# Sample attention: who loads the pages, when the choice of blocks and two exponentials run, and when the first output weights are asked for

## The reference

```python
s_c = einsum(qg, kc); p_c = masked_softmax(s_c)        # compressed branch, 127 tokens a sequence
imp = where(causal, where(forced, 1e9, einsum(p_c, sel_map)), NEG)
_, idx = lax.top_k(imp, 16)                            # choice: 16 of 33 blocks of 64 tokens
o_s = softmax(qg @ K[idx]) @ V[idx]                    # selected branch, pages through page_table
o_w = softmax(qg @ K_win) @ V_win                      # window of 512
o = g[0] * o_c + g[1] * o_s + g[2] * o_w
h = x + concat(o, o_rwkv) @ w_out
```

## Time and profile before

| | |
|---|---|
| median of 3 runs | 2213.54 us (2210.96 to 2214.94) |
| the profiled execution's own time | 2216.07 us |
| its span, first to last instruction | 2214.3 us |
| PE busy | 2114.0 us (95%) |
| mean granted clock of TensorE | 0.976 of full |
| sample attention, first turn to first product of the output projection | 1111.76 to 1242.97 us of the span |

### The profile page before, as it was taken

The page is one execution under the profiler, slowest core; times in us unless marked ns, Lnnn a source line. Parts: engine busy times, 40 slices in busy tenths (PEclk is TensorE's granted clock), DMA queues, the critical chain, the costliest instruction groups (busy, mean ns, idle before and its releaser), DMA issues.

```text
span 2214.3 us, 37125 instructions
## 1 busy us (share of the span) xinstructions
PE 2114.0 (95%) x15276; PEld 1199.3 (54%) x15276; DVE 1130.4 (51%) x2310; ACT 627.7 (28%) x1411; POOL 150.8 (7%) x248
## 2 busy tenths in 40 slices
PE   8999999899998998999987899999999999999999
PEld 6445556799996784444443444444444444444443
DVE  2035654467665547776555114453635455453635
ACT  5014542222222125766643222202011111111020
POOL 3000000122221001212100000000000000000000
PEclk9999999999997997999988899999999999999999
DMA  6001113101012621000045320111111111111112
GB/s 177 37 0 29 29 28 100 50 4 23 4 23 79 199 69 54 10 6 10 1 148 158 99 101 33 38 38 38 38 38 38 38 38 38 38 38 38 39 38 81
DMA packets 99958, 115.73 MB, mean 52 GB/s; under 512 B 32243, under 2 KB 72116, under 8 KB 99726
## 3 DMA queue, kind: packets, MB, share of 16 engines
q1 hardware_dynamic: 95310, 106.01, 15.2%
q10 hardware_dynamic: 4480, 7.34, 1.2%
HBM read 104.75 MB, written 12.64 MB: 53 GB/s over the span
## 4 chain that ended last, share of the span: by engine, by line
PE 86%; DVE 5%; ACT 4%; SPq 2%; issue 2%; DMA 1%; ACTq 0%; POOL 0%; POOLq 0%; DVEq 0%
PE psum L1352 80%; PE psum L1800 2%; PE psum L1684 1%; SPq L742 1%; ACT arena L1235 1%; ACT arena L1221 1%; PE psum L1857 1%; DVE arena L2422 1%; DVE arena L2448 1%; DVE arena L2272 1%; PE psum L1602 0%; PE psum L1362 0%; SPq L688 0%; ACTq L1186 0%; PE psum L2045 0%
## 5 line engine op out<-in xcount | busy, mean ns | idle before, releaser
L1352 PE MATMUL psum<-arena 64*64 64x64 f32 (+10 forms) x12320 | 1864.8, 350 | 57.5 <-ACT arena L1235 20.3
L1352 PEld LDWEIGHTS psum<-arena 64*64 64x64 f32 (+5 forms) x12320 | 970.1, 152 | 844.6 <-issue 667.6
L2602 DVE TENSOR_TENSOR arena<-arena,psum 128x512 f32<-128x512 f32 x48 | 33.0, 688 | 306.2 <-PE psum L1352 306.2
L1333 ACT ACTIVATE arena<-psum 128x512 f32<-128x512 f32 x48 | 28.5, 594 | 419.9 <-PE psum L1352 327.3
L1324 ACT ACTIVATE arena<-arena 128x512 f32<-128x512 f32 x64 | 40.2, 628 | 274.2 <-DVE arena L2612 168.0
L896 POOL TENSOR_TENSOR arena<-arena,m_lev 128x256 f32<-128x256 f32 x82 | 65.4, 798 | 575.0 <-DVE arena L2253 377.6
L1221 ACT ACTIVATE arena<-psum 128x512 f32<-128x512 f32 (+1 forms) x148 | 80.7, 596 | 69.2 <-PE psum L1800 60.6
L2422 DVE TENSOR_REDUCE arena<-psum 128x1 f32<-128x640 f32 (+7 forms) x128 | 84.6, 703 | 15.1 <-PE psum L1352 13.6
L1235 ACT ACTIVATE arena<-psum,arena 128x640 f32<-128x640 f32 (+7 forms) x128 | 89.0, 703 | 11.6 <-DVE arena L2422 11.5
L1800 PEld LDWEIGHTS psum<-ident,arena 128*128 128x128 f32 x528 | 58.2, 144 | 45.8 <-issue 22.4
L2272 DVE TENSOR_TENSOR arena<-arena,psum 128x512 f32<-128x512 f32 x65 | 44.6, 686 | 74.2 <-PE psum L1352 73.5
(11 more groups left out here) (312 smaller groups left out, 1743.2 us busy)
## 6 DMA issues: line engine op xcount, KB each, us to landing
arena<-in_cache_slc_kv_dram SPq DMA_DIRECT2D x128, 128.0 KB, 2.3
arena<-in_w_up_dram SPq DMA_DIRECT2D x7, 2048.0 KB, 7.4
arena<-in_w_down_dram SPq DMA_DIRECT2D x7, 2048.0 KB, 7.9
arena<-in_cache_cmp_kv_dram SPq DMA_DIRECT2D x72, 128.0 KB, 3.3
arena<-in_x_prompt_dram SPq DMA_DIRECT2D x16, 512.0 KB, 5.7
arena<-in_cache_cmp_kv_dram ACTq DMA_DIRECT2D x56, 128.0 KB, 3.2
arena<-in_w_in_dram SPq DMA_DIRECT2D x13, 512.0 KB, 3.6
arena<-in_w_in_dram SPq DMA_DIRECT2D x2, 2048.0 KB, 12.6
```

The source lines that it names most:

```text
L1352: return nc.tensor.matmul(out, lhsT, rhs, start=start, stop=stop)
L2602: tt(u2, t_sb, bank_of(6), ALU.add).then_inc(sem("u_sum"), 1)
```

## The change

1. SP loads the pages of sequences 4 and 6 only. POOL, after its work in prompt attention, loads those of 5 and 7 from its own queue: for each four pages it reads the numbers, waits for `sg_o`, and issues; after 16 it waits until they have landed. PE waits for them on a new semaphore, `ctok_in_pool`.
2. SP asks for the first two parts of `w_out` after the last `s_weigh` of a page group of the last pair; for the other two it waits for `sa_o` as before.
3. The head sum and the turn for the choice stand in step 1 of a front, in place of step 3.
4. In backs 0 and 2, ACT makes the exponential of the other pair's selected branch after its copies of "v" and "t" and not ahead of the window's exponential.
5. The `vb` products of the 17th RWKV chunk stand at k = 1, behind the `tu` products, in place of k = 4. The turns of the 16th chunk's result (`o_pe`, k = 1) come between them and the `nub` products.
6. `pa_c_out` is gone; the compressed strip counts in `pa_max` twice, and the waits are renumbered.

```diff
 # SP
-                numbers = [batch_pages(b) for b in (2 * p_, 2 * p_ + 1)]
-                for b in (2 * p_, 2 * p_ + 1):
-                    for n in range(NPG):
-                        if n % 4 == 0:
-                            sp.wait_ge(sem("sg_o"), pslot["p", p_ - 2, n // 4] + 1)
-                        load_page(b, n, numbers[b % 2][n])
+                numbers = batch_pages(2 * p_)
+                for n in range(NPG):
+                    if n % 4 == 0:
+                        sp.wait_ge(sem("sg_o"), pslot["p", p_ - 2, n // 4] + 1)
+                    load_page(2 * p_, n, numbers[n])
...
-            sp.wait_ge(sem("sa_o"), DEC_B // 2)
+            sp.wait_ge(sem("sg_o"), pslot["p", NPAIR - 1, 3] + 1)
             for q, (k0, _) in enumerate(WO_ORDER):
+                if k0 == 0:
+                    sp.wait_ge(sem("sa_o"), DEC_B // 2)
 # POOL, at its end
+            for b in range(5, DEC_B, 2):
+                for n in range(NPG):
+                    if n % 4 == 0:
+                        numbers = [nc.gpsimd.value_load(pages[0:1, b * NPG + n + x:b * NPG + n + x + 1]) for x in range(4)]
+                        pool.wait_ge(sem("sg_o"), pslot["p", b // 2 - 2, n // 4] + 1)
+                    src = cache_slc_kv[0, bass.ds(numbers[n % 4], 1)].rearrange("o s a g d -> (o s) a (g d)")
+                    nc.gpsimd.dma_start(page_at(b, n), src).then_inc(sem("ctok_in_pool"), 16)
+                pool.wait_ge(sem("ctok_in_pool"), 16 * NPG * (b // 2 - 1))
 # ACT
-                act.wait_ge(sem("pa_max"), exps[x] + g + 1)
+                act.wait_ge(sem("pa_max"), 2 * x + (2 if s == "c" else g + 1))
...
-                    if n % 2 == 0:
-                        s_exp(n + 1)
                     act.wait_ge(sem("sw_max"), n + 1)
...
                     s_copy("v", n, 0)
                     s_copy("t", n, 0)
+                    if n % 2 == 0:
+                        s_exp(n + 1)
 # PE
-                if k == 4:
                     if c == NCH:
                         pe.wait_ge(*once("rw_vb"))
...
+                if k == 4:
                     pe.wait_ge(sem("rw_nu"), c + 1)
...
-                    pe.wait_ge(sem("pa_c_out"), steps_s[compressed][0] // 2 + 1)
+                    pe.wait_ge(sem("pa_max"), 2 * compressed + 1)
...
                     if q == 0:
-                        pe.wait_ge(sem(f"ctok_in{b % 4}"), 16 * NPG * (b // 4 + 1))
+                        if b >= 4 and b % 2:
+                            pe.wait_ge(sem("ctok_in_pool"), 16 * NPG * (b // 2 - 1))
+                        else:
+                            pe.wait_ge(sem(f"ctok_in{b % 4}"), 16 * NPG * (b // 4 + 1))
...
-                    if j == 3:
+                    if j == 1:
                         pe.wait_ge(sem("sc_pn"), p_ + 1)
 # DVE
-                    ins.then_inc(sem("pa_c_out"), 1)
-                    dve.wait_ge(sem("pa_c_out"), i + 1)
+                    ins.then_inc(sem("pa_max"), 1)
+                    dve.wait_ge(sem("pa_max"), 2 * x + 1)
```

## The result

| | before | after |
|---|---|---|
| median (lowest to highest) of 4 runs each | 2214.24 us (2210.96 to 2215.22) | 2190.3 us (2186.85 to 2193.48) |
| ratio, 95% interval | | 0.9897 (0.9875 to 0.9919) |
| profiled execution's own time, span | 2216.07, 2214.3 | 2193.48, 2191.9 |
| sample attention begins | 1111.76 | 1111.64 |
| from there to the first turn for the MLP | 162.69 | 140.37 |

I call the stretch of the last row "the stage": sample attention and the first two tiles of the output projection. What follows it took 939.85 us before (2214.3 - 1274.45) and 939.89 after (2191.9 - 1252.01), so in these two profiles all 22.3 us (162.69 - 140.37) lie inside it.

What follows compares the result with a forecast made beforehand. PE, busy for 95% of the span, was taken as the bound, with waits in sample attention to remove. 1.9 + 5.8 + 7.4 + 2.95 = 18.05, less 0.9 for late pages: 2213.54 - 17.1 = 2196.4 us, range 2192 to 2211.

Steps and rivals of the forecast that it cites:

- the step on the exponentials' order: Backs 0 and 2: the window's exponential starting sooner wins 3.0 us of waiting and 2.8 of clock, 5.8 together.
- the 7.4 of the pages: Front 3: with pages in time it lasts 15.7 us like front 1, not 23.1, so 7.4 is won.
- Choice: Fronts 0 and 2: the mask's gap behind them shrinks, winning 0.6 and 1.3 us, 1.9 together; clock left as it was.
- For u = 1.2 it lands at 1193.2: 0.9 late: Front 3, step 4: at u = 1.2 us of POOL per page, sequence 7 lands 0.9 us after PE wants it.
- Output weights: Ahead of the output projection: `w_out` requested 2.95 us sooner, so 2.95 of PE's 3.95 us wait is won.
- Not counted: Output projection: the lower clock behind the `w_out` gap might not come, 3 us more, left out of the sum.
- Edits at nothing: RWKV's moved `vb` products and prompt attention's renumbered waits: no gain; lost cover of `nub` would cost at most 2 to 3 us.
- A: Rival, page loads: POOL issues slowly, saving 55.5 - 32u (u: us per page), nothing at 1.74; 12% above that, 4% for 1.6 to 1.74.
- B: Rival, page loads: POOL takes 1.3 to 1.6 us a page, saving 4.5 to 14, about 9: 2204.5 us; chance 21%.
- C: Rival, PE's clock: it is not given back or drops elsewhere, saving 14.3 us: 2199; chance 18%.
- D: Rival, page loads: the DMA engines limit them, costing front 3 up to 4 us for sequence 6: 2200; chance 8%.

Runs made afterwards that it cites:

- fine: The changed kernel with odd fronts starting on the first `ss_add` count, other counts awaited bank by bank, their head sum in step 3: 2186.59 us, ratio 0.9883.
- fill: The changed kernel with three products whose result nobody reads on PE in the gap ahead of fronts 1 and 3: 2186.47 us, ratio 0.9884.
- no_pages: The changed kernel with the pages of sequences 5 and 7 back on SP's queue: 2198.16 us, ratio 0.9944 to the kernel before.
- no_exp: The changed kernel with the big exponential ahead of the window's again in backs 0 and 2: 2198.63 us, ratio 0.9943 to the kernel before.
- no_wout: The changed kernel with all four parts of `w_out` asked for after `sa_o`: 2193.43 us, ratio 0.9926 to the kernel before.
- slow_pool: The changed kernel with a memset on POOL, and its wait for it, ahead of each page load: 2217.97 us, ratio 1.0023 to the kernel before.
- fine2: The kernel fine with ACT's exponential of the compressed scores behind its copy of step 2 in odd fronts: 2181.47 us, ratio 0.9864 to the kernel before.
- rwkv_only: The kernel before with only the `vb` products of the 17th RWKV chunk moved to k = 1: 2207.92 us, ratio 0.9979.

## Why the prediction was off

Of the 17.1 forecast, 3.9 were clock: 2.8 in the step on the exponentials' order, and 1.1 that stood unnamed inside the 7.4 of the pages, whose comparison of fronts 3 and 1 has 1.1 of busy time in it (16.80 - 15.66). The other 13.2 were idle time. The stage gave 22.3: 15.0 idle and 7.3 clock. So 3.4 of the 5.2 missed in the stage are clock and 1.8 idle.

**Idle time: the mechanisms right, two sizes off.**
- Choice: 0.6 and 1.3 forecast, 0.5 and 1.2 measured; the wait of 0.7 at the sum and the mask as what is late next are both there.
- Exponentials: 3.0 forecast, 3.3 measured (1.5 and 1.7).
- Pages: 5.4 forecast (7.4 less 1.1 of clock and 0.9 of late pages), 6.3 of waiting went. The step "For u = 1.2 it lands at 1193.2: 0.9 late" failed twice, in opposite directions: u was 0.91, and the landing of sequence 5 took 7.4 and not 2.7. Nothing was late.
- Output weights: 2.95 forecast, 3.8 measured. I kept the 5.8 us from the request to the projection. It took 4.9 at most, and PE did not wait (4.9 to 5.4, with waits of 0.3 to 0.7, in fine, fill, no_pages and no_exp). The attention parts were asked for 2.9 us after the first request and not 1.6 as before, so they shared the engines less; that this is the reason was not tested.

**The clock: the step that failed.** The sum had 2.8 for it, in the step on the exponentials' order, 1.1 inside "With pages in time 7.4 is won", and "Not counted" for the projection; 3.9 in all, and 7.3 came. It was in the backs (4.0 where 2.8 were taken; the stretch from the turn of "v" to the next weights, 7.78 and 6.75 before, took 5.64 and 5.65, which is 3.2 of it), in front 3 (2.1 where 1.1 stood) and in the projection (1.5 where nothing was counted), less 0.3 lost in front 1. The trace of the kernel before had shown it: the clock was 0.75 in front 3 and 0.91 in the projection's first tiles, each behind a gap that the change takes away. I should have priced every gap taken away with its length and the slow stretch behind it. The experiments show both halves: no_exp costs 5.0 idle and 7.1 clock, no_wout 3.7 and 1.5, and fill wins 3.1 by clock alone, with every gap of 2.8 us still as long but filled. Only at the choice was leaving the clock alone right.

**The range.** Its lower end, 2192, took all terms at full: 2213.54 less 21.05, of which 14.1 were idle and 6.9 clock (2.8, 1.1, and 3 for the projection). The stage gave 22.3, by 0.9 more idle and 0.3 more clock: 2191.2. The kernel before stood at 2214.24 with the fourth run, 0.7 higher: 2191.9. The last 1.6, down to 2190.3, lie outside the stage. So even the best case was short at the output weights' wait, and it left no room for the scatter of the stage's start, 6 us from one execution to another, which medians of four runs keep a part of. It was an end made of one best case, and not of the bounds of what was unknown.

**Edits at nothing.** Edit 6 shows no cost. Edit 5 is worth 0 to about 2 us and not nothing: the order of the same products decided how soon the clock rose among them. The medians differ by 23.9 and the stages by 22.3; the 1.6 between are within the reach of this and of the scatter of the start, and no run parts the two.

**Rivals.** A (slow POOL) was decided by u = 0.91; slow_pool shows its line right within some 3 us (6.3 by the line, 9.3 in the stage, 5.1 in the times). B fell with u. C was wrong in its sign: the clock gave back more than was taken. D's mechanism was there and hidden with 1.2 to 1.5 us to spare; fine2 uses them up. Four pages took POOL 2.30 us to issue beside DVE's ranking (1173.72) and with DVE nearly idle (1162.71), so no lock-out by DVE showed; but DVE made no float32 copy from SBUF to SBUF at those times, the case that the prediction names, so that case stays untested.

## What to carry to other kernels

Split a stage into PE's idle time and its busy time: when the instructions are the same, the second difference is the clock, and it can be a third of a gain. Price a gap at its length plus the slow stretch behind it, look for work to fill a gap that can't be closed, and do not expect edits to add up: a queue that is late takes up what is won ahead of it, so its own edit is worth 3 to 7 us alone and 13.6 us last. When a wait is split finer, look at what stands behind the next in-order engine before counting the gain.

## What was not expected of the hardware

- POOL issues a plain load of a 128 KB page in 0.55 to 0.61 us (2.30 to 2.42 for four), as fast as SP (17.66 for 32), also while DVE ranks blocks; between two groups of four, with four number reads from SBUF, pass 1.33 us.
- With both queues issuing, the DMA engines were busy for 0.98 of 16 us at 302 GB/s, and a sequence's pages landed 7.4 us after the last issue in place of some 2.7.
- The lower clock falls on different instructions of RWKV in different executions of the same program (224 products in 6.87 or 9.6 us), and the start of sample attention moves by up to 6.6 us (1105.17 and 1111.76), nearly all of it PE's busy time in the kernel before. The stage itself repeated within 0.3 us for both kernels; in rwkv_only, whose stage is that of the kernel before, it took 5.2 more.
- Products with no use in two gaps of 2.8 us kept the clock at 1.00 over 137 us.
